# Small inputs issued later, setup moved behind the second tile, one table load and two weight waits in the first stage of a decoder layer kernel

## What is computed

```python
def rms_norm(x, g):
    xf = x.astype(jnp.float32)
    xf = xf * lax.rsqrt(jnp.mean(xf * xf, axis=-1, keepdims=True) + EPS)
    return xf.astype(x.dtype) * g

def project_in(x, ln1, w_in):
    z = jnp.einsum('bsd,de->bse', rms_norm(x, ln1), w_in)
    offs = np.cumsum((0,) + IN_SPLITS)
    u, q, k, v, qi, ki, wi, gates = [z[..., offs[i]:offs[i + 1]] for i in range(len(IN_SPLITS))]
    ...

# in attend: a bias by distance bucket and head is added to the logits
bias = rel_bias[rel_bucket(jnp.maximum(dist, 0))].astype(jnp.float32)
```

## Time and profile before

| | |
|---|---|
| time, median of 3 runs | 1810.98 us (1809.92 to 1811.01) |
| profiled execution | 1810.34 us |
| its span | 1808.6 us |
| TensorE busy | 1689.4 us (93%) |
| VectorE busy | 767.3 us (42%) |
| ScalarE busy | 458.3 us (25%) |
| GpSimd busy | 407.0 us (23%) |

### The profile page before, as it was taken

One profiled execution on the slowest core, in us unless ns is written; L12 is line 12 of the kernel. 1 busy time (PEld: TensorE's weight loads), 2 busy tenths in 40 slices (PEclk: granted clock), 3 DMA queues, 4 the chain that ended last, 5 costly groups with the idle time before them and its releaser, 6 DMA issues.

```text
span 1808.6 us, 25066 instructions
## 1 busy us (share of the span) xinstructions
PE 1689.4 (93%) x9820; PEld 1407.8 (78%) x9820; DVE 767.3 (42%) x1882; ACT 458.3 (25%) x860; POOL 407.0 (23%) x351
## 2 busy tenths in 40 slices
PE   4998699989999898779999999999999999999997
PEld 2554266646666555568889999999999999999996
DVE  2214899999200455342144443313313313313325
ACT  1213211253112554331133321121121121121113
POOL 3000205411111432011112242232232232232220
PEclk9996899999999899989999999999999999999999
DMA  5500411260111332032221121111111111111002
GB/s 156 113 26 1 153 63 36 79 247 18 35 38 38 140 141 94 13 100 59 66 70 47 60 81 47 47 46 46 46 46 46 46 46 46 46 46 46 0 1 106
DMA packets 114687, 116.91 MB, mean 65 GB/s; under 512 B 17310, under 2 KB 103982, under 8 KB 112557
## 3 DMA queue, kind: packets, MB, share of 16 engines
q1 hardware_dynamic: 102471, 73.74, 13.7%
q0 software_dynamic: 4160, 39.33, 6.5%
q10 hardware_dynamic: 7982, 2.83, 0.6%
HBM read 107.66 MB, written 8.45 MB: 64 GB/s over the span
## 4 chain that ended last, share of the span: by engine, by line
PE 55%; DVE 1%; DMA 1%; ACT 1%; issue 0%; DVEq 0%; ACTq 0%
PE banks L108 52%; PE banks L1538 3%; DMA out_dram<-yo 0%; PE banks L1519 0%; DVE yo L1856 0%; DVE XL L1769 0%; DMA raw<-in_w_in_dram 0%; ACT XH L1682 0%; DVE rinv L1821 0%; ACT junk L1759 0%; ACT hT L1679 0%; ACT sH L1673 0%; PE banks L1615 0%; PE banks L1561 0%; DVE gated L1776 0%
## 5 line engine op out<-in xcount | busy, mean ns | idle before, releaser
L108 PE MATMUL banks<-hnH,wH 128*128 128x344 f32 x1056 | 339.0, 321 | 3.8 <-DVE sg L1830 3.8
L108 PE MATMUL banks<-hnH,wL 128*128 128x344 f32 x1056 | 337.8, 320 | 0.0
L494 PE MATMUL banks<-hT,big 128*128 128x344 f32 x768 | 226.9, 457 | 1.3 <-ACT I L977 0.7
L494 PEld LDWEIGHTS banks<-hT,big 128*128 128x128 f32 x768 | 147.3, 192 | 79.0 <-issue 2.4
L108 PEld LDWEIGHTS banks<-hnH,wH 128*128 128x128 f32 x1056 | 199.4, 189 | 4.4 <-issue 4.3
L1647 POOL TENSOR_TENSOR wL<-w_raw,wH 128x1024 fp32r<-128x1024 f32 (+1 forms) x55 | 155.8, 2851 | 204.2 <-ACT wH L1709 203.9
L108 PEld LDWEIGHTS banks<-hnH,wL 128*128 128x128 f32 x1056 | 199.2, 189 | 0.0
L1844 DVE TENSOR_TENSOR hT<-hT,banks 128x344 f32<-128x344 f32 x264 | 135.2, 513 | 107.1 <-PE banks L108 107.0
L108 PE MATMUL banks<-aH,wH 128*128 128x344 f32 x528 | 169.3, 321 | 1.6 <-DVE hT L1844 1.6
L108 PE MATMUL banks<-aH,wL 128*128 128x344 f32 x528 | 169.7, 321 | 0.0
L108 PE MATMUL banks<-hnL_lo,wH 128*128 128x344 f32 x528 | 169.1, 320 | 0.0
(11 more groups left out here) (287 smaller groups left out, 2621.1 us busy)
## 6 DMA issues: line engine op xcount, KB each, us to landing
w_raw<-in_w_gate_up_dram SPq DMA_DIRECT2D x44, 512.0 KB, 3.9
w_raw<-in_w_down_dram SPq DMA_DIRECT2D x11, 1024.0 KB, 4.9
big<-in_w_in_dram SPq DMA_DIRECT2D x12, 512.0 KB, 3.9
W<-in_x_prompt_dram SPq DMA_DIRECT2D x8, 512.0 KB, 4.5
raw<-in_w_in_dram SPq DMA_DIRECT2D x8, 512.0 KB, 5.0
x_nat<-in_x_prompt_dram SPq DMA_DIRECT2D x8, 512.0 KB, 4.0
raw<-in_w_out_dram SPq DMA_DIRECT2D x8, 512.0 KB, 3.8
out_dram<-yo SPq DMA_DIRECT2D x8, 512.0 KB, 2.6
```

The costliest lines, as they stand in the source:

```text
L108: last = nc.tensor.matmul(out, w_cols(w, k), x_cols(x, k), start=(k == 0 and j == 0), stop=(k == nk - 1 and j == 2))
L494: last = mm(ps[:, bank, 0:CH], big[:, s, k, :], hT[:, k, c * CH:(c + 1) * CH], start=k == 0, stop=k == KD - 1)
```

## The change

- ScalarE issues only ln1's DMA at the start, on a semaphore of its own, ln1_in. The other eleven small DMAs are issued behind stats(2), ahead of natural_out(0), on consts_in.
- Before stats(0), ScalarE takes one root of the constant eps (one element a partition). It raises x_root by one, so VectorE's scale_x(t) waits for one more.
- VectorE waits for ln1_in before hT_out(0). The setup from inputs, with its wait for consts_in, stands behind hT_out(2), ahead of naturalT_out(0).
- w_kv and w_ix have a semaphore each. TensorE waits for w_kv before the first group of natural(0), and for w_ix before the second.

```diff
@@ -266,7 +266,7 @@
             ri = sb("ri", [P, NH])
 
             x_in = [sem(f"x_in{b}") for b in range(3)]
-            consts_in = sem("consts_in"); nat_w_in = sem("nat_w_in")
+            ln1_in = sem("ln1_in"); consts_in = sem("consts_in"); kv_w_in = sem("kv_w_in"); ix_w_in = sem("ix_w_in")
             consts_made = sem("consts_made"); poolw_in = sem("poolw_in"); upto_made = sem("upto_made")
             x_squared = sem("x_squared"); x_root = sem("x_root"); x_scaled = sem("x_scaled"); rstd_ready = sem("rstd_ready")
             xT_ready = sem("xT_ready"); hT_ready = sem("hT_ready")
@@ -301,7 +301,7 @@
 
             block = ctx.enter_context(nc.Block())
             U_ITEMS, Q_ITEMS = 4, 4
-            N_CONST_DMA = 3 + 1 + NB
+            N_CONST_DMA = 2 + 1 + NB
 
             PAIRS = 4 * NBLK
 
@@ -346,8 +346,8 @@
             def _(sp):
                 for t in range(3):
                     sp.dma_start(x_ring[0:rows(t), t, :], xp[tile_cols(t), :]).then_inc(x_in[t], 16)
-                sp.dma_start(w_kv, w_in_t[:, :, C_K:C_K + NKVC]).then_inc(nat_w_in, 16)
-                sp.dma_start(w_ix, w_in_t[:, :, C_QI:C_QI + NIDX]).then_inc(nat_w_in, 16)
+                sp.dma_start(w_kv, w_in_t[:, :, C_K:C_K + NKVC]).then_inc(kv_w_in, 16)
+                sp.dma_start(w_ix, w_in_t[:, :, C_QI:C_QI + NIDX]).then_inc(ix_w_in, 16)
                 for t in range(3, NT):
                     sp.wait_ge(xT_ready, 2 * (t - 3) + 2)
                     sp.dma_start(x_ring[0:rows(t), t % 3, :], xp[tile_cols(t), :] if t < NBLK else xs)\
@@ -412,12 +412,14 @@
 
                     r = rows(t)
                     if t == 0:
-                        pe.wait_ge(nat_w_in, 32)
+                        pe.wait_ge(kv_w_in, 16)
                     pe.wait_ge(hT_ready, 2 * t + 2)
                     if t >= 2:
                         pe.wait_ge(nat_evac, t - 1)
                     for k in range(KD):
                         mm(ps[0:r, 4 + t % 2, 0:NKVC], hT[:, k, tile_cols(t)], w_kv[:, k, :], start=k == 0, stop=k == KD - 1)
+                    if t == 0:
+                        pe.wait_ge(ix_w_in, 16)
                     for k in range(KD):
                         last = mm(ps[0:r, 6 + t % 2, 0:NIDX], hT[:, k, tile_cols(t)], w_ix[:, k, :], start=k == 0, stop=k == KD - 1)
                     last.then_inc(nat_ready, 1)
@@ -888,7 +890,9 @@
             def _(act):
                 A = nc.scalar.activation
                 with nc.allow_non_contiguous_dma(reason="small vectors laid out by partition"):
-                    act.dma_start(ln1c[:, :], ln1[0].rearrange("(k p) -> p k", p=P)).then_inc(consts_in, 16)
+                    act.dma_start(ln1c[:, :], ln1[0].rearrange("(k p) -> p k", p=P)).then_inc(ln1_in, 16)
+
+                def small_inputs():
                     act.dma_start(ln2c[:, :], ln2[0].rearrange("(k p) -> p k", p=P)).then_inc(consts_in, 16)
                     act.dma_start(pscl[:, :], pool_scale[0].rearrange("(k p) -> p k", p=P)).then_inc(consts_in, 16)
                     act.dma_start(pta[:, 0:NBUCKETS * NH], bass.AP(rel_bias.tensor, 0, [[0, P], [1, NBUCKETS * NH]])).then_inc(consts_in, 16)
@@ -925,11 +929,16 @@
                     act.dma_start(dst[2], kst[0:r, b, 512:576]).then_inc(nat_out[b], 16)
 
                 act.wait_ge(pool_fill, 1)
+                A(stat[:, 1, 0:1], eps[:, :], ACT.Sqrt).then_inc(x_root, 1)
+                act.wait_ge(x_root, 1)
                 stats(0)
                 stats(1)
                 for t in range(NT):
                     if t + 2 < NT:
                         stats(t + 2)
+                    if t == 0:
+                        with nc.allow_non_contiguous_dma(reason="small vectors laid out by partition"):
+                            small_inputs()
                     natural_out(t)
 
 
@@ -1086,7 +1095,7 @@
 
                 def scale_x(t):
                     r = rows(t)
-                    dve.wait_ge(x_root, t + 1)
+                    dve.wait_ge(x_root, t + 2)
                     V.reciprocal(stat[0:r, 2, t:t + 1], stat[0:r, 1, t:t + 1]).then_inc(rstd_ready, 1)
                     dve.wait_ge(rstd_ready, t + 1)
                     V.tensor_scalar(x_ring[0:r, t % 3, :], x_ring[0:r, t % 3, :], stat[0:r, 2, t:t + 1], None, ALU.mult).then_inc(x_scaled, 1)
@@ -1119,25 +1128,29 @@
                 dve.wait_ge(setup_step, 2)
                 V.tensor_scalar(last_lane[:, :], last_lane[:, :], 1.0, -NONCAUSAL, ALU.subtract, ALU.mult).then_inc(setup_step, 1)
 
-                dve.wait_ge(consts_in, 16 * N_CONST_DMA)
-                dve.wait_ge(pool_fill, 2)
-                V.tensor_tensor(own_head, table, fold8.unsqueeze(1).to_broadcast([P, NBUCKETS, NH]), ALU.mult).then_inc(setup_step, 1)
-                dve.wait_ge(setup_step, 4)
-                V.tensor_reduce(rb[:, :], own_head, AX.X, ALU.add).then_inc(setup_step, 1)
-                V.tensor_scalar(sub_m[:, :], sub_i[:, :], SR - 1, None, ALU.bitwise_and).then_inc(setup_step, 1)
-                dve.wait_ge(setup_step, 6)
-                V.tensor_copy(sub_f[:, :], sub_m[:, :]).then_inc(setup_step, 1)
-                dve.wait_ge(setup_step, 7)
-                V.tensor_scalar(rowid[:, :], pti[:, :], float(SR), sub_f[:, :], ALU.mult, ALU.add).then_inc(setup_step, 1)
+                def setup_from_inputs():
+                    dve.wait_ge(consts_in, 16 * N_CONST_DMA)
+                    dve.wait_ge(pool_fill, 2)
+                    V.tensor_tensor(own_head, table, fold8.unsqueeze(1).to_broadcast([P, NBUCKETS, NH]), ALU.mult).then_inc(setup_step, 1)
+                    dve.wait_ge(setup_step, 4)
+                    V.tensor_reduce(rb[:, :], own_head, AX.X, ALU.add).then_inc(setup_step, 1)
+                    V.tensor_scalar(sub_m[:, :], sub_i[:, :], SR - 1, None, ALU.bitwise_and).then_inc(setup_step, 1)
+                    dve.wait_ge(setup_step, 6)
+                    V.tensor_copy(sub_f[:, :], sub_m[:, :]).then_inc(setup_step, 1)
+                    dve.wait_ge(setup_step, 7)
+                    V.tensor_scalar(rowid[:, :], pti[:, :], float(SR), sub_f[:, :], ALU.mult, ALU.add).then_inc(setup_step, 1)
 
                 scale_x(0)
                 scale_x(1)
+                dve.wait_ge(ln1_in, 16)
                 hT_out(0)
                 for t in range(NT):
                     if t + 2 < NT:
                         scale_x(t + 2)
                     if t + 1 < NT:
                         hT_out(t + 1)
+                    if t == 1:
+                        setup_from_inputs()
                     if t >= 1:
                         naturalT_out(t - 1)
                 naturalT_out(NT - 1)
```

## The result

The changed kernel took 1795.85 us in the median of 6 runs (1791.29 to 1801.81), the kernel before 1811.74 beside it: a ratio of 0.9917, 95% interval 0.9895 to 0.9939. Forecast were 1798.3, from 1795.0 to 1802.3. Over all sets, the executions of the changed kernel spread over 16 us, those of the kernel before over 13. Medians and ratios leave out four executions in a slower state: one of 2464.53 us (mean granted clock 0.65) with the small inputs first, and three of 1869 to 1874 us with a spare product behind every head. Most of what follows is about the spread.

A forecast was written before the change was run, and what follows sets the result against it. TensorE's waits in the first slice, behind small transfers, were taken as the bound. Gains of 13.7 - 1.0 + 0 = 12.7 us took 1810.34 to 1797.6; the median lies 0.64 above: 1798.3 us, range 1795.0 to 1802.3.

The forecast's parts named there:

- The front: TensorE's first projection, held by w_kv's landing, starts at 14.4 (bounds 13.0 to 14.8) instead of 28.08: 13.7 us gained.
- The reading that leaves the start at 14.65: Skill text: all issuers' transfers share the same 16 DMA engines, so w_kv lands no sooner for moving small inputs.
- The cold start: Tile 0's first 16 projections run partly at TensorE's lower clock: 1.0 us lost, bounds 0.5 gained to 3.5 lost.
- Rival 1: Half of tile 0's first 16 matmuls run at 1.2 GHz: 3.5 us lost instead of 1.0, 1800.8 us; chance 0.15.
- The small inputs: ScalarE's moved issues end near 22, before its evacuation at 27.4; VectorE's setup near 34 waits for none: no cost.
- The bias transfer: bias_rows, issued at 46, stalls TensorE 1.9 us in a later tile, replacing the old 1.88: net 0, bounds -1.9 to +3.
- The sum of the tile loop: 13.7 at the front, less 1.0 for the clock, plus 0 for bias_rows: the loop ends 12.7 us earlier.
- I take a shift of the end of the tile loop as a shift of the end of the kernel: Stages behind the tile loop move as a block, so its 12.7 us reach the kernel's end; argued from the waits.
- its allowance of 1 us either way for the clock: Later stages: an earlier start may place the granted clock's dips otherwise, 1 us more or less.
- the forecast's own sign of being wrong: Wrong if w_kv lands after 15, small issues run past 33, or loop end and kernel end move by different amounts.
- rival 3: The bias_rows transfer misses TensorE's path altogether: 1.9 us less, 1796.4 us; chance 0.12.

The follow-up runs named there:

- the two further sets: The changed kernel run again twice with no edit: medians 1790.46 us (ratio 0.9876) and 1794.57 us (0.9891).
- the shift: Changed kernel plus two extra products (1.71 us) in tile 6, so the scores start 1.7 us later: 1801.29 us, ratio 0.9936.

## Why the forecast was right, and where it was lucky

- **The front.** Forecast was a first projection at 14.4 and a gain of 13.7 there; it was 14.03 and 14.05. w_kv landed at 2.24 + 11.7 = 13.94, 0.7 sooner than in the kernel before, where 0.25 had been taken out of at most 0.7: inside the bounds of 13.0 to 14.8. The reading that leaves the start at 14.65 did not hold. The order of arrival was as worked out: root 0 at 6.06 (6.15), second transposes at 11.07 (11.1), w_kv last, w_ix no wait.
- **The cold start.** 1.0 lost was taken; the first 16 took 8.58 us against 7.59 in the earlier trace rows, 0.99 more (1.11 and 1.44 in the two further profiles). Rival 1 did not come. That TensorE is at its lower level there is read from durations: the profile's granted clock says 1.00 over the whole first slice, also where eight transposes take 1.94 us. Behind the first gather, at 178.89, eight such transposes take 1.94 us again, and there the granted clock reads 0.50.
- **The small inputs.** ScalarE was through at 19.06, 3 us earlier than forecast: issuing took 9.2 us instead of the 12 of the earlier trace rows. The setup started at 33.31 (34) without a wait. Its cover was real, and the experiment with the setup first shows what it costs without.
- **The bias transfer.** Forecast: issued at 46, a stall of 1.9 at tile 5's transposes in place of the old one, then a held evacuation that costs nothing. Seen: issued at 43.66, a stall of 1.40 at 66.31, an evacuation held 6.15 us at 81.40 with no idle on TensorE. Net 0.48 gained instead of 0.
- **The sum of the tile loop.** 12.7 was forecast, 13.55 measured in the profile: 14.05 at the first projection, less 0.99, plus 0.48.
- **The step that failed** is "I take a shift of the end of the tile loop as a shift of the end of the kernel", with its allowance of 1 us either way for the clock. The row that could have warned stood in the earlier trace rows: the clock reads 6 in the slice of the scores. The profiled kernel gave back 2.8 us in the scores and 2.3 later (8.5 at the end), so the forecast's own sign of being wrong, that the loop's end moves by another amount than the kernel's, came true. The medians of the three sets gained 2.3, 8.5 and 5.9 us more than the front. The allowance had to be near 10 us, the 46.0 less 35.5 that separate a stage with and without its slow stretch.
- **Luck.** That the first median fell in the range is owed to the front's accuracy and to the clocks of those six executions. The medians of the two further sets, 1790.46 and 1794.57, lie below the range, which ends at 1795.0; on either of them the same forecast would have missed. Two small slips of the working change nothing: the range's end by its own terms (rival 3, w_kv 0.9 sooner) is 1795.5, and the loop's end 141.81 - 12.7 = 129.1, not 129.5.

Why the changed kernel finds the upper level more often than the kernel before (0.981 to 0.983 in 4 of 16 executions, none of 42 above 0.979) stays open. The variants without early root, with the inputs first, with the setup first, with the bias held back and with the shift did not show it in 4, 8, 10, 10 and 4 executions; the one with the weights together did once in 4. The three profiles of one kernel show that the slow stretch changes at nearly the same start, 128.26 to 128.63; whether the start matters too, no run here separates. What the runs do show is that the gap ahead of the scores counts: filled, the profiled clock held through the stage, and all four executions were at 0.981 or more, against 4 of 16 without.

## What to carry to other kernels

Look at the first slice of a busy kernel by itself, and list for its first large product every arrival in order: a small load does its harm not by its bytes but by the queue of the engine that issues it and of the engine that waits for it. If its issue is moved back, what waits for it has to move back too. After a gain at the front, compare not only the end, but each later stage's length and granted clock; here a stage of the same instructions took 42.4 to 46.2 us, and 35.5 with four small products more. Time a version several times and set the times against the mean granted clock before a difference of 5 us is given to an edit.

## What the runs showed of the hardware

- A short idle stretch can cost much more than itself. In the changed kernel TensorE stood 2.1 us in three pieces (1.14, 0.42 and 0.57) between 128.3 and 133, and the clock fell at 133.1; with four spare products between 128.9 and 134.3, some 3 us by their durations, it stayed at 2.4 GHz through the stage, which took 10.5 us less.
- In the profiles a full TensorE does not get its clock back soon in this stage: 33.27 us busy of 34.1 at 0.50 in the changed kernel, 50.00 of 50.00 at 0.50 with a spare product per head. In the tile loop the same engine rose within its first 16 projections (8.58 us, where the next 16 take 7.03). The Trainium skill, TensorE: Matmul & The Clock Gate, Part 1, says that the array is throttled when idle and released by sustained activity. The first half agrees with these runs; for the second, the rows of this stage differ, and the measurement decides: busy time alone is not what brings it back. What does is not settled here.
- While the transfer of bias_rows runs (1.5 MB out of 8 partitions, 37.2 us), four of the six issues of output DMAs on ScalarE's queue take 3.2 to 4.6 us instead of 0.34 to 0.48, in the kernel before and in the changed one; the first of the six still takes 0.38 and 0.34. It does not do so everywhere. Held back to 127.71, the transfer runs beside the three output issues of the 8 sample rows, and these take 0.54, 0.29 and 0.32 us. What of the load makes the difference is not shown.
